# The chunked two-way scan of an RWKV-style mixer: its triangular inverse as a counted loop on TensorE, in four array tiles

## The chip, the core and the metric

One core of one Trainium2 chip runs one program: two layers of a first block and one layer of a second block, all in fp32. The metric is device time in microseconds (us). The kernel before takes 3105.51 us, the median of 3 runs (3105.34 to 3112.76). The profiled execution took 3111.09 us, with a span of 3109.3 us.

## The reference, cut to what matters

The change touches only the recurrence of the second block: 16 heads of 64 channels, two directions (forward and backward in time), 256 context tokens and then 256 tokens of x, the state carried from one to the other.

```python
def wkv_scan(s0, scan_in):
    def step(s, inp):
        w, kk, a, k, v, r = inp          # decay, removal key, rate, key, value, receptance
        sa = jnp.einsum('dbhij,dbhj->dbhi', s, kk)
        s = s * w[..., None, :] - sa[..., :, None] * (kk * a)[..., None, :] + v[..., :, None] * k[..., None, :]
        return s, jnp.einsum('dbhij,dbhj->dbhi', s, r)
    return lax.scan(step, s0, scan_in)

s_ctx, y_c = wkv_scan(s0, scan_c)        # context: only the state is used
_, y_x = wkv_scan(s_ctx, scan_x)         # x: the outputs are used
```

## The kernel before

**Chunks.** The scan goes in 8 steps of 64 tokens, 4 of context and 4 of x. In a step both directions run side by side, so there are 32 chains (16 heads, 2 directions). A buffer such as `Pm`, `Qm` or `LT` is 128 x 1024: its two partition halves are the two heads of a pair, and its columns are 2 directions x 8 pairs x 64. Inside a chunk the recurrence is solved with 64x64 matrices. `Qm` and `Pm` are the decayed removal keys, `Km` the decayed keys, `Rm` the receptances. `LT` is their masked product, `Apk`, `Arq` and `Ark` are the other masked products, and `Kt`, `Qt` and `VT_TOK` are the keys and values turned to token-major by a product with the identity.

**The inverse.** The inverse of the unit triangular matrix and its transpose are held in `Dm` and `DTm` and grow by doubling blocks (level masks for block sizes 1, 2, 4, ... 32). The first level is made from `LT` and from a second product `L` by masks alone. Five levels follow, each with three products per direction: `AL` = masked left matrix `Loff` times `Dm`, copied out by ACT to `ARm`; `E` and `ET`, which DVE subtracts from `Dm` and `DTm`. DVE also makes the next level's `Loff` from `LT`.

**Products on TensorE.** `product()` (L1623) opens one PSUM bank per direction, waits for its operands and issues 8 pairs x 2 heads matmuls of 64x64 by 64. fp32 makes each of them two weight loads and two matmul instructions. A head reads its own partition half and writes the same half of the bank, so of the four 64x64 tiles of the array only the two on the diagonal are used, in turn. One direction of one product, here called a bank, is 32 matmul instructions.

**Order.** `head()` (L1655) makes a step's products and inverse, `tail()` (L1676) the values `U0`, the corrected values `U`, the outputs `Y` (x only) and the state `St`. Each engine runs its own program, in order. PSUM goes through two rings of 4 banks, one emptied by ACT and one by DVE, and a bank is opened when its last user has freed it. The 8 steps are written as loops on each engine (`pe.Fori(0, 3)` at L1696 for context, `pe.Fori(0, 2)` at L1705 for x) with straight code around them; the PE loop body is a whole step. The next step's rates are made inside the inverse: `rate_sums` on DVE, `sigmoids` (L1913) on ACT, two running sums `cumulate` on DVE (after levels 1 and 2), `decays` (L1918) on ACT, and then six products on DVE for `Qm`, `Pm` and `Km`. GpSimd (POOL) copies two small inputs per step (L2582, L2588). Since two scan buffers lie where x is, x is written to HBM before the scan and read back after it.

Of the kernel before, what the change touches and what calls it, by code (L numbers as in the profile page):

```python
# [13 lines left out]
P = 128  # L14
# [24 lines left out]
def sections(*parts):  # L39

    out, at = {}, 0
    for name, passes, per in parts:
# [6 lines left out]
SECTIONS_ACT = sections(("layers", LAYERS, 92), ("attention", 1, 120), ("scan_first", 1, 16), ("scan_ctx", 3, 20),  # L49
                        ("scan_turn", 1, 20), ("scan_x", 2, 20), ("scan_end", 1, 20), ("scan_last", 1, 4))  # L50
SECTIONS_DVE = sections(("layers", LAYERS, 64), ("attention", 1, 28), ("scan_first", 1, 32), ("scan_ctx", 3, 32),
                        ("scan_turn", 1, 36), ("scan_x", 2, 36), ("scan_end", 1, 32), ("scan_last", 1, 4))
# [74 lines left out]
def constants2():  # L127
# [23 lines left out]
    put("level", np.tile(np.stack(levels, 1), (2, 1, 1, 1)))  # L151
# [105 lines left out]
class PsumRing:  # L257
# [31 lines left out]
    def peek(self, eng, section, tag, k):  # L289

        n = [i for i, t in enumerate(self.filled[section]) if t == tag][k]
        eng.wait_ge(self.full, self.count(section, 0, n))
        return self.banks[:, n % 4, :]

# [26 lines left out]
def build_program(nc, W1, V1, K1, W2_all, VV2, K2, R2, PU, PV, xin, cin, out):  # L321
# [931 lines left out]
    css2, csd2, crs2 = sm2[:, 108:110], sm2[:, 110:112], sm2[:, 112:114]  # L1253
    ys, yd, yr = sm2[:, 120:152], sm2[:, 152:184], sm2[:, 184:216]
# [18 lines left out]
    lor = rb(256).rearrange("p (d s t) -> p d s t", d=2, s=2)  # L1273
# [7 lines left out]
    Z = [sb2(1024, slots_at + 1024 * i) for i in range(14)] + [sb2(1024, 1024 * i) for i in range(2)] + [rb(1024) for _ in range(7)]  # L1281
    assert slots_at + 14 * 1024 <= base - nv2 - ncon2 - ncon and rtop[0] <= MEM_COLS, rtop[0]
    r0, r1, r2, r3, Pm, nU, Rm, ARm, Loff, U0, Qm, Km, Dm, DTm, VT_TOK, _, Kt, Qt, Apk, Ark, Arq, LT, St = Z
# [5 lines left out]
    Vt = r3  # L1289

# [22 lines left out]
    def pb(n):  # L1313
# [62 lines left out]
    shifted_ready, lora_act_ready = signal("shifted_ready"), signal("lora_act_ready")  # L1376
    kk_sq_ready, kk_root_ready, scan_ready = signal("kk_sq_ready"), signal("kk_root_ready"), signal("scan_ready")

    step_in_ready, values_in_ready = signal("step_in_ready"), signal("values_in_ready")
    inputs_used = signal("inputs_used")  # L1380
    lora_sums_ready, rates_ready = signal("lora_sums_ready"), signal("rates_ready")
    cumsum_ready, decays_ready = signal("cumsum_ready"), signal("decays_ready")
    pq_ready, k_ready, r_ready = signal("pq_ready"), signal("k_ready"), signal("r_ready")
    intra_ready, tokens_ready = signal("intra_ready"), signal("tokens_ready")
    level_left_ready, inverse_ready, inverseT_ready = (
        signal("level_left_ready", 10), signal("inverse_ready", 10), signal("inverseT_ready", 12))
    u0_ready, u_ready = signal("u0_ready", 2), signal("u_ready", 2)
    state_ready = signal("state_ready")
    x_back = sem("x_back")
    scan_done_act, scan_done_dve = sem("scan_done_act"), sem("scan_done_dve")  # L1390
# [6 lines left out]
    idx_used = sem("idx_used")  # L1397
# [11 lines left out]
    def _(sp):  # L1409
        sp.dma_start(rows2, R2.rearrange("p (m n) -> p m n", m=2)).then_inc(rows_landed, 16)  # L1410
        sp.dma_start(ctxs, cin.rearrange("(t p) n -> p t n", p=P)).then_inc(ctx_landed, 16)
        for n, (name, count) in enumerate(ITEMS2):
            if n == LAST_BEFORE_SCAN + 1:

                sp.wait_ge(shift_parts_ready.sem, 1)
                sp.dma_start(lora, W2[:, w2_total:w2_total + 2048]).then_inc(lora_landed, 16)

                sp.wait_ge(*xn2_ready.at(0, 0))
                sp.dma_start(out.rearrange("(t p) n -> p t n", p=P), x).then_inc(stored, 16)
                sp.wait_ge(scan_done_act, 1)  # L1420
                sp.wait_ge(scan_done_dve, 1)
            if n == LAST_BEFORE_SCAN + 3:
                sp.wait_ge(stored, 16)
                sp.dma_start(lora[:, 0:1024], W2[:, w2_total + 2048:w2_total + 3072]).then_inc(lora_landed, 16)
                sp.dma_start(x, out.rearrange("(t p) n -> p t n", p=P)).then_inc(x_back, 16)
# [12 lines left out]
        sp.wait_ge(stored, 48)  # L1438
# [3 lines left out]
    def _(pe):  # L1442
# [163 lines left out]
        def stand():  # L1606

            pe.sem_inc(pe_step, 1)

        def section(name):  # L1610
            act_ring.pe_section = dve_ring.pe_section = name

        def operand(buf, head, chain):

            rows_ = slice(64 * head, 64 * head + 64)
            if buf is None:
                return ident[rows_, rows_]
            return ch(buf)[rows_, chain, :]

        def product(ring, it, tag, *terms, ready=None):  # L1620


            for d in range(2):  # L1623
                b = ring.open(pe, it, tag)
                if ready is not None:
                    for r in ready(d):
                        pe.wait_ge(*r)
                stand()
                for c in range(8):
                    for head in range(2):  # L1630
                        for i, (lhsT, rhs) in enumerate(terms):
                            last = mm(b[64 * head:64 * head + 64, c * 64:(c + 1) * 64], operand(lhsT, head, 8 * d + c),
                                      operand(rhs, head, 8 * d + c), i == 0, i == len(terms) - 1, skip=True)
                last.then_inc(ring.full, 1)

        def rates(it, h):

            pe.wait_ge(*step_in_ready.at(h))
            stand()
            for d in range(2):  # L1640
                for c in range(8):
                    if c % 4 == 0:
                        b = dve_ring.open(pe, it, "lora")
                        stand()
                    last = mm(b[:, (c % 4) * P:(c % 4 + 1) * P], lora[:, d * D + c * P:d * D + (c + 1) * P],
                              lor[:, d, :, :].rearrange("p s t -> p (s t)"), True, True)
# [987 lines left out]
```

## Time and profile before

| | |
|---|---|
| median of 3 runs | 3105.51 us |
| profiled execution, its span | 3111.09 us, 3109.3 us |
| busy: PE, DVE, ACT, POOL | 2772.7, 1450.2, 571.7, 333.4 us |
| mean granted TensorE clock | 0.941 |
| 64x64 matmul instructions in the scan | 14080, 444.3 us |
| the scan, from its last setup memset to its last state product | 1690 to 2217 us |

A step of the scan can be timed by any instruction that comes once in it. A row of groups gives busy time, the mean duration of one instruction, and the idle time of the engine before them with what ended it. A row of windows gives each engine's busy time and instruction count in a stretch, and the clock granted to TensorE (1.0 is 2.4 GHz, 0.5 is 1.2 GHz).

### The profile page before, as it was taken

How to read it: one execution, taken by the hardware profiler on the slowest of the kernel's cores; microseconds unless marked ns; L12 is line 12 of the kernel's file. 1: busy time of each engine (PE TensorE's matmuls, PEld its weight loads, DVE VectorE, ACT ScalarE, POOL GpSimd, SP SyncE). 2: the span in 40 equal slices, each digit the busy share in tenths (PEclk: the TensorE clock that was granted, in tenths of full speed). 3: DMA queues.
4: the chain of work that ended last, by engine and by line, in shares of the span. 5: the costliest groups of instructions: out<-in, count | busy, mean ns of one | idle time of the engine just before them, and what ended most of it. 6: DMA issues, size and time to landing. Idle time of an engine off the chain costs nothing.

```text
span 3109.3 us, 54722 instructions
## 1 busy us (share of the span) xinstructions
PE 2772.7 (89%) x22658; PEld 1942.1 (62%) x22658; DVE 1450.2 (47%) x3078; ACT 571.7 (18%) x1254; POOL 333.4 (11%) x310
## 2 busy tenths in 40 slices
PE   8997799899978998999996899999898887878777
PEld 6786586477865853444686898989785633333332
DVE  2635200135352001054363777777412687777754
ACT  1241100013320000114222333222100211111111
POOL 0000000000000000000000000000000255444452
PEclk9998999998989999999998999999999999898898
DMA  4322243242223344313420000000333699999996
GB/s 182 136 82 85 105 163 149 108 177 107 86 82 125 146 162 179 142 72 119 154 94 1 4 4 4 4 4 4 130 136 122 263 422 421 421 421 422 421 421 287
DMA packets 55639, 510.22 MB, mean 164 GB/s; under 512 B 6112, under 2 KB 6112, under 8 KB 8032
## 3 DMA queue, kind: packets, MB, share of 16 engines
q0 software_dynamic: 37024, 269.12, 20.9%
q1 hardware_dynamic: 18368, 237.51, 20.0%
q8 instruction: 191, 3.13, 0.4%
q14 instruction: 56, 0.46, 0.0%
HBM read 504.51 MB, written 2.10 MB: 163 GB/s over the span
## 4 chain that ended last, share of the span: by engine, by line
PE 31%; DMA 11%; DVE 7%; PEld 5%; issue 3%; ACT 1%; DVEq 1%; POOL 0%; PEldq 0%; ACTq 0%; POOLq 0%; SPq 0%
PE psum L1453 28%; DMA mem<-weights,mem 11%; PEld psum L1453 5%; DVE mem L2522 3%; PE psum L1792 2%; DVE mem L2027 2%; DMA mem<-weights 1%; POOL mem L2601 0%; PE psum L1463 0%; ACT mem L2012 0%; ACT mem L2007 0%; DVE mem L2450 0%; DVE mem L2483 0%; DVE mem L2442 0%; DVE mem L2444 0%
## 5 line engine op out<-in xcount | busy, mean ns | idle before, releaser
L1453 PE MATMUL psum<-mem 64*64 64x64 f32 (+5 forms) x16792 | 1120.0, 253 | 93.8 <-issue 39.8
L517 PE MATMUL psum<-mem 128*128 128x256 f32 (+8 forms) x4228 | 1067.5, 421 | 25.6 <-DVE mem L1174 12.9
L1453 PEld LDWEIGHTS psum<-mem 64*64 64x64 f32 (+3 forms) x16792 | 887.3, 145 | 322.1 <-issue 244.5
L517 PEld LDWEIGHTS psum<-mem 128*128 128x128 f32 (+3 forms) x4228 | 769.2, 196 | 317.1 <-issue 227.1
L1792 PE MATMUL psum<-mem 128*128 128x512 f32 x1024 | 507.0, 655 | 134.2 <-ACT mem L2012 133.9
L1792 PEld LDWEIGHTS psum<-mem 128*128 128x128 f32 x1024 | 210.3, 210 | 430.2 <-issue 252.1
L2601 POOL DMA_INDIRECT mem<-weights,mem x256 | 313.0, 1223 | 610.5 <-PE psum L1792 289.3
L2522 DVE CUSTOM_DVE_ANT_0 mem<-mem 128x1024 f32<-128x1024 f32 x256 | 307.9, 1224 | 145.3 <-DMA mem<-weights,mem 140.0
L2027 DVE TENSOR_TENSOR mem<-mem 128x512 f32<-128x512 f32 (+4 forms) x378 | 268.3, 727 | 119.2 <-ACTq L1848 82.7
L2027 DVE TENSOR_TENSOR mem<-psum,mem 128x512 f32<-128x512 f32 (+3 forms) x178 | 99.0, 585 | 175.9 <-PE psum L1453 156.3
L1908 ACT ACTIVATE mem<-psum 128x512 f32<-128x512 f32 x160 | 95.5, 597 | 341.3 <-PE psum L1453 341.3
L2027 DVE TENSOR_TENSOR mem<-mem,psum 128x512 f32<-128x512 f32 x148 | 101.5, 687 | 63.2 <-PE psum L1453 49.2
L2582 POOL COPY mem<-mem 64x64 f32 x32 | 9.5, 298 | 1088.7 <-DVEq L2224 1081.8
L1198 DVE TENSOR_TENSOR mem<-mem 128x512 f32<-128x512 f32 x32 | 22.2, 693 | 202.9 <-ACTq L914 202.9
L535 PE MATMUL psum<-mem 128*128 128x128 f32 (+2 forms) x390 | 55.7, 304 | 67.5 <-DVEq L1152 33.9
L994 DVE SCALAR_TENSOR_TENSOR mem<-mem 128x256 f32<-128x256 f32 x240 | 105.6, 481 | 10.5 <-issue 1.8
L2007 ACT ACTIVATE mem<-mem 128x4 f32<-128x4 f32 x64 | 13.1, 205 | 506.9 <-DVE mem L2526 506.9
L1202 DVE TENSOR_TENSOR mem<-psum,mem 128x512 f32<-128x512 f32 x8 | 5.5, 692 | 212.9 <-PE psum L517 212.9
L535 PEld LDWEIGHTS psum<-mem 128*128 128x128 f32 (+2 forms) x390 | 50.3, 152 | 74.8 <-issue 72.9
L2012 ACT ACTIVATE mem<-mem 128x128 f32<-128x128 f32 x256 | 81.8, 390 | 29.9 <-DVE mem L2027 29.4
L776 ACT ACTIVATE mem<-psum 128x512 f32<-128x512 f32 (+5 forms) x94 | 48.5, 570 | 108.2 <-PE psum L517 102.9
L1212 POOL DMA_DIRECT2D mem<-vectors x2 | 1.3, 646 | 607.8 <-DVEq L1203 606.9
(218 smaller groups left out, 1037.4 us busy)
## 6 DMA issues: line engine op xcount, KB each, us to landing
mem<-weights SPq DMA_DIRECT2D x102, 2048.0 KB, 7.3
mem<-weights SPq DMA_DIRECT2D x2, 2176.0 KB, 7.9
mem<-weights,mem POOLq DMA_INDIRECT x256, 22.2
mem<-weights SPq DMA_DIRECT2D x2, 1536.0 KB, 7.5
mem<-weights SPq DMA_DIRECT2D x3, 1024.0 KB, 9.3
mem<-weights SPq DMA_DIRECT2D x2, 1152.0 KB, 8.1
mem<-weights SPq DMA_DIRECT2D x2, 1120.0 KB, 5.1
mem<-x SPq DMA_DIRECT2D x1, 1024.0 KB, 5.9
```

The source lines that it names most:

```text
L517: ins = pe.matmul(out, lhsT, rhs, start=start, stop=stop, skip_group_check=skip)
L535: last = pe.transpose(b[0:rows_, at:at + n], src, ident[0:n, 0:n])
L776: return A(dst, src(b) if src else b, func).then_inc(act_ring.free, 1)
L994: v.scalar_tensor_tensor(cacc[:, c, :], src, w, cacc[:, c, :], ALU.mult, ALU.add)
L1198: v.tensor_tensor(f, f, f, ALU.mult).then_inc(ff_ready.sem, 1)
L1453: ins = pe.matmul(out, lhsT, rhs, start=start, stop=stop, skip_group_check=skip)
L1792: last = pe.matmul(psum[:, 4 + 2 * t + half, :], diag[:, n % DIAGS, :], rows_uv[n % NBUF][:, D + half * 512:D + (half + 1) * 512], start=k ...
L1908: done(A(dst[:, d * 512:(d + 1) * 512], take(tag, it), ACT.Copy, scale=scale))
L2012: A(diag[:, n % DIAGS, :], ident, ACT.Copy, scale=g1[:, n:n + 1]).then_inc(diag_ready.sem, 1)
L2027: return v.tensor_tensor(o, a, b, op)
L2522: v.tensor_tensor_reduce(u, u, h2[:, t, :], 1.0, 0.0, ALU.mult, ALU.add, actp[:, n:n + 1])
L2601: pool.indirect_dma_start(out=rows_uv[n % NBUF], out_offset=None, in_=UV, in_offset=bass.IndirectOffsetOnAxis(ap=eidx_u[:, n:n + 1], axis= ...
```

## The change

The steps are written out on every engine; the outer loops go. What is a loop now is the inverse, on TensorE alone: six turns, one per level, for each of the 8 steps. The other engines' code for the six levels is written out.

Let h be the step. The left matrix is no longer masked before the product: `LT` minus the identity (subtracted by POOL) is multiplied by `Dm` in all six levels, and DVE puts the level's mask (now minus the mask, with the diagonal kept) on the product as it leaves PSUM. The new `Dm` and `DTm` are then plain products, copied out of PSUM. They begin as identities, and the `L` product goes. Operands and results now change partition halves, so that the two products of a level fall on all four array tiles.

```diff
+        def tile(b, d, c, head, swapped_in, swapped_out, lhsT, rhs, first=True, last=True):
+            side, out = head ^ swapped_in, head ^ swapped_out
+            return mm(b[64 * out:64 * out + 64, c * 64:(c + 1) * 64], lhsT(side, d, c), rhs(side, d, c), first, last, skip=True)
...
+            with pe.Fori(0, LEVELS) as j:
+                for d in range(2):
+                    pe.wait_ge(inverse_ready.sem, j * 2 + ((2 * LEVELS - 2) * h + d + 1))
...
+                            last = tile(left[d], d, c, head, 0, 1, half_of(LT), half_of(Dm))
+                    last.then_inc(left_full.sem, 1)
+                for d in range(2):
+                    pe.wait_ge(left_ready.sem, j * 2 + (2 * LEVELS * h + d + 1))
+                    pe.wait_ge(inverseT_ready[d].sem, j + ((LEVELS - 1) * h + 1))
...
+                            one = tile(products[d][0], d, c, head, 1, 0, half_of(DTm), half_of(ARm))
+                            two = tile(products[d][1], d, c, head, 1, 1, half_of(ARm), half_of(DTm))
+                    one.then_inc(inverse_full.sem, 1)
+                    two.then_inc(inverseT_full.sem, 1)
```

On DVE and ACT, per level (`between` is where the next step's rates go: `cumulate` after levels 0 and 1, with the wait for the sigmoids in front of the first):

```diff
+            for j in range(LEVELS):                      # DVE
+                for d in range(2):
+                    v.wait_ge(*left_full.at(h, 2 * j + d))
+                    tt(dir_(ARm, d), left[d]..., bc(level[:, j, 1 - d, :], 1, 8), ALU.mult)
+                    v.drain().then_inc(left_ready.sem, 1)
+                if j < LEVELS - 1:
+                    v.wait_ge(*inverseT_full.at(h, 2 * j + 1))
+                    v.tensor_copy(DTm[:, 512:1024], banks)
+                    v.drain().then_inc(inverseT_ready[1].sem, 1)
+                between(j)
...
+                        if j == 0:
+                            v.wait_ge(*rates_ready.at(h + 1))
+                        cumulate(j)
+                    if j == 1:
+                        exclude()
...
+            for j in range(LEVELS):                      # ACT
+                for d in range(2):
+                    if j < LEVELS - 1:
+                        act.wait_ge(*inverse_full.at(h, 2 * j + d))
+                        A(Dm[:, d * 512:(d + 1) * 512], banks[2 * d], ACT.Copy)
+                        act.drain().then_inc(inverse_ready.sem, 1)
+                    if j == LEVELS - 1 or d == 0:
+                        act.wait_ge(*inverseT_full.at(h, 2 * j + d))
+                        A(DTm[:, d * 512:(d + 1) * 512], banks[2 * d + 1], ACT.Copy)
...
+                between(j)          # j == 0: sigmoids(h + 1); 2: first_decays(h + 1); 3: later_decays()
```

The key products become 128 columns wide: one weight load of `Qm` (or `Km`) meets `Pm` and the identity in one matmul, giving `LT` and `Qt` (or `Apk` and `Kt`). Two of them with different tiles are interleaved (`together`). `U0`, `Y` and `St` are cut into phases that put terms of the two directions on different tiles; between phases PE waits for its own last matmul (`term_full`). `Ark` and `Arq` are interleaved in the same way. The rates are two products with 64 rows each instead of one with 128.

```diff
+        def wide(bank, d, c, head, swapped_out, lhsT):
+            out = head ^ swapped_out
+            to = bank[64 * out:64 * out + 64, :].rearrange("p (b n) -> p b n", b=2)[:, :, 64 * (c % 4):64 * (c % 4) + 64]
+            return mm(to, lhsT(head, d, c), removal_and_unit(head, d, c), True, True, skip=True)
...
+        for h in STEPS:
+            read = h - 1 in X_STEPS
+            if read:
+                y = first_outputs(h - 1)
+            else:
+                together(removal(h, 0))
+            if h:
+                corrected_values(h - 1)
+            if read:
+                last_outputs(h - 1, y)
+            if h:
+                state_update(h - 1)
+            values_product(h)
...
+            together(removal(h, 1), keys(h, 0))          # where not read; where read: both directions in pairs
+            together(keys(h, 1))
+            pe.wait_ge(*qt_ready.at(h, 1))
+            if h < 7:
+                for d in range(2):
+                    rates(h + 1, d)
+            uncorrected(h)
+            if h in X_STEPS:
+                reads(h)
+            inverse(h)
```

`Qm`, `Pm` and `Km` are now made by POOL, with a two-instruction form of the key factor:

```diff
+                pool.wait_ge(*rates_ready.at(h + 1))
...
+                removal_raw(h + 1)      # Qm = kk * r1                 (2 products of 128x512)
+                key_factors()           # r1 = r1 * k_a + (1 - k_a)    (4)
+                removal_keys(h + 1)     # waits decays_ready; Qm *= r2 (128x1024), Pm = kk * r3 (2); then pq_ready
+                keys_raw(h + 1)         # r1 *= zk                     (2)
+                keys(h + 1)             # Km = r1 * r2 (128x1024); then k_ready
```

After the last step the state is no longer updated. Two fewer scan buffers are needed, so x stays in place and its trip to HBM and back goes.

## Rows read from the trace of the kernel before

**Rows 1.** Windows, the whole core: five steps of the scan, then their columns.
```profile
core 0: us, PE busy (x) PEld busy (x) DVE busy (x) ACT busy (x) POOL busy (x), PEclk, DMA share, GB/s
1793.00:1852.84 59.84, 54.51 (x1639) 53.42 (x1636) 43.01 (x68) 19.46 (x27) 2.09 (x6) 0.94 0.02 4
...
1913.70:1974.65 60.95, 58.13 (x1768) 56.11 (x1765) 46.82 (x74) 19.36 (x26) 2.46 (x6) 1.00 0.02 4
1974.65:2041.38 66.73, 63.63 (x1956) 61.82 (x1954) 48.33 (x76) 19.36 (x27) 2.09 (x6) 1.00 0.02 4
```

**Rows 2.** Groups by shape in 1670 to 2215 us, all engines.
```profile
L1453 PE MATMUL psum<-mem 64*64 64x64 f32 x14080 | 444.3, 221 | 46.1 <-issue 39.8 <-DVE mem L2027 2.7
...
L2027 DVE TENSOR_TENSOR mem<-mem,psum 128x512 f32<-128x512 f32 x144 | 99.0, 687 | 63.2 <-PE psum L1453 49.2 <-issue 8.4 <-PEq L1688 1.0
L1908 ACT ACTIVATE mem<-psum 128x512 f32<-128x512 f32 x160 | 95.5, 597 | 341.3 <-PE psum L1453 341.3
...
L2027 DVE TENSOR_TENSOR mem<-mem 128x1024 f32<-128x1024 f32 x31 | 38.1, 1229 | 3.7 <-issue 1.3
...
L2272 DVE TENSOR_TENSOR_SCAN mem<-mem 128x512 f32<-128x512 f32 x16 | 19.5, 1223 | 6.5 <-ACT mem L1915 3.5 <-issue 2.1
L1915 ACT ACTIVATE mem<-mem 128x2048 f32<-128x2048 f32 x8 | 15.3, 1911 | 0.1
```

**Rows 3.** Timeline of ACT: the table load that comes once per step (start, duration).
```profile
1737.05 1.28 ACT L1915 ACT_TABLE_LOAD   x1 [0.18 <-issue]
1791.69 1.28 ACT L1915 ACT_TABLE_LOAD   x1 [0.25 <-issue]
...
1973.36 1.28 ACT L1915 ACT_TABLE_LOAD   x1 [0.18 <-issue]
2040.09 1.28 ACT L1915 ACT_TABLE_LOAD   x1 [0.24 <-issue]
```

**Rows 4.** Timeline of one level: an evacuation, then PE's first weight load after it.
```profile
1922.68 0.60 ACT L1908 ACTIVATE mem<-psum 128x512 f32<-128x512 f32 x1 [4.58 <-PE psum L1453]
...
1923.63 0.69 PEld L1453 LDWEIGHTS psum<-mem 64*64 64x64 f32 x20 [0.19 <-issue]
```

**Rows 5.** Windows: 64x64 products, the rates, and narrow products in the first block.
```profile
1902.00:1905.50 3.50, 3.50 (x128) 3.50 (x124) 2.96 (x6) 2.39 (x4) 0.00 (x0) 1.00 0.02 5
1905.67:1909.20 3.53, 3.53 (x35) 3.53 (x32) 2.67 (x8) 0.60 (x1) 0.00 (x0) 1.00 0.02 5
...
173.54:173.80 0.26, 0.26 (x18) 0.26 (x18) 0.26 (x1) 0.15 (x1) 0.00 (x0) 1.00 0.45 189
```

**Rows 6.** Groups by shape in 173.4 to 174.3 us: the narrow products.
```profile
L517 PE MATMUL psum<-mem 128*15 128x64 f32 x16 | 0.5, 222 | 0.0
```

**Rows 7.** Loop lines of PE (L1696) and DVE (L2363): duration least, median, most.
```profile
L1696 PEldq COMPARE_BRANCH  x3: 83/3360/3378, 1818.2 to 1939.0; - x3
...
L2363 DVEq COMPARE_BRANCH  x3: 50/67/74, 1819.0 to 1939.9; - x3
```

**Rows 8.** Windows around the first taken branch of the context loop on PE.
```profile
1817.40:1822.00 4.60, 0.16 (x6) 0.05 (x2) 1.74 (x5) 3.32 (x4) 0.00 (x0) 0.74 0.01 4
1822.00:1824.00 2.00, 2.00 (x37) 2.00 (x39) 1.80 (x4) 0.00 (x0) 0.00 (x0) 0.50 0.04 8
...
1826.00:1828.00 2.00, 2.00 (x68) 2.00 (x66) 0.40 (x1) 0.35 (x2) 0.00 (x0) 0.90 0.03 8
```

**Rows 9.** POOL's groups by shape.
```profile
L2588 POOL COPY mem<-mem 128x512 f32 x16 | 9.3, 608 | 433.5 <-DVEq L2315 433.5
```

**Rows 10.** Timeline at both ends of the scan.
```profile
1690.00 0.07 DVE L2219 MEMSET mem<- 128x8 f32 x1
...
1711.11 0.17 DVE L2297 COPY mem<-mem 128x8 f32<-128x8 f32 x1 [4.71 <-ACT mem L1924]
...
1735.33 0.60 ACT L1908 ACTIVATE mem<-psum 128x512 f32<-128x512 f32 x1 [4.26 <-PE psum L1453]
...
2215.53 1.23 DVE L2027 TENSOR_TENSOR mem<-mem 128x1024 f32<-128x1024 f32 x1
```

More of the change, by code:

```diff
@@ L293, in peek, with held @@
         return self.banks[:, n % 4, :]
+    def held(self, count):
+        tags = self.emptied[self.section]
+        tags.extend(["held"] * count)
+        return [self.banks[:, n % 4, :] for n in range(len(tags) - count, len(tags))]
     def check(self, section):
@@ L1605, in _ @@
         pe.wait_ge(*scan_ready.at(0))
[L1606 to L1620, printed above, removed]
-            for d in range(2):
[L1624 to L1628, printed above, removed]
+        act_ring.pe_section = dve_ring.pe_section = "post"
@@ L1634, in product, with corrected_values @@
[L1634 to L1639, printed above, removed]
+                        last = tile(b, d, c, head, 0, 1, values(h), unit)
+                last.then_inc(act_ring.full, 1)
+        def corrected_values(h):
+            for d in range(2):
+                b = act_ring.open(pe, 0, "U")
+                pe.wait_ge(*inverse_done.at(h, d))
+                pe.wait_ge(*u0_ready.at(h, d))
+                for c in range(8):
+                    for head in range(2):
+                        last = tile(b, d, c, head, 1, 0, half_of(DTm), half_of(U0))
+                last.then_inc(act_ring.full, 1)
@@ new lines, in output_terms @@
+        def output_terms(h, b, phases):
+            terms = ((0, half_of(Rm), half_of(St)), (1, half_of(Ark), half_of(VT_TOK)), (0, half_of(Arq), half_of(nU)))
+            for phase in phases:
+                for c in range(8):
+                    for head in range(2):
+                        for d, i in phase:
+                            swapped, lhsT, rhs = terms[i]
+                            last = tile(b[d], d, c, head, swapped, 0, lhsT, rhs, i == 0 and c == 0, i == 2)
+                if phase[-1][1] == 2:
+                    last.then_inc(dve_ring.full, 1)
+                else:
+                    pe.wait_ge(term_full.sem, mark(last))
@@ new lines, in keys, with together @@
+        def keys(h, d):
+            b = [act_ring.open(pe, 0, "K") for _ in range(2)]
+            return lambda c, head: wide(b[c // 4], d, c, head, 1, half_of(Km)), act_ring
+        def together(*products):
+            for c in range(8):
+                for head in range(2):
+                    last = [product(c, head) for product, _ in products]
+                if c % 4 == 3:
+                    for ins, (_, ring) in zip(last, products):
+                        ins.then_inc(ring.full, 1)
@@ L1640, in rates, with reads @@
+        def reads(h):
+            b = [[dve_ring.open(pe, 0, n) for n in ("Arq", "Ark")] for _ in range(2)]
             for d in range(2):
                 for c in range(8):
[L1642 to L1646, printed above, removed]
@@ L1959, in _ @@
+        corrected_values()
+        act.sem_inc(scan_done, 1)
         act.wait_ge(*y_var_ready.at(0))
```

584 lines of the change are left out of this document (328 added, 256 removed).

## The prediction

> **What bounds the kernel now.** The slices and the chain of waits on the page say that PE is busy nearly everywhere; outside the scan the change moves only one transfer. So I read the scan alone: windows by step, groups by shape, then the timeline of one level. PE's records cover 63.6 of 66.7 us of a step of x [rows 1], but a busy PE is not a full one. The dense row holds 128 matmul instructions in 3.50 us, 27 to 29 ns each [rows 5] (records missing or cut at the edges allow both; I use 29.2, and 0.93 us for a bank of 32). A context step without a taken branch takes 54.64 us, a step of x 66.73 [rows 3]. A context step has 50 banks (12 in the head, 28 in the inverse, 10 in the tail): 46.7 us. Its rates are 32 instructions of 128 columns, 3.53 us [rows 5]. Together 50.2 of 54.6 us: PE's instruction stream is the bound, hand-offs cost 4.4 us a step. DVE is busy 43 to 48 us and ACT 19 [rows 1]; both wait for PE [rows 2].
>
> **Array tiles.** Each 64x64 instruction takes 2 x 29.2 = 58 ns of its tile, and two tiles alternate. Do four go at once? No 64x64 product shows it, but narrow ones do: 18 instructions in 0.26 us, 14.4 ns each [rows 5], nearly all of one kind, 64 moving columns into 15 output partitions [rows 6], which go to four column groups in turn. That is four times the rate of one tile. I take 14.6 ns for products on four tiles. Bounds: 14.6, and 29.2 if the row halves or the issue don't allow it.
> The Trainium skill, TensorE: Matmul & The Clock Gate (Back-to-back issue gap), says that matmuls never start less than about 25 ns apart on average. The short burst above goes below it, but 18 instructions can come out of a queue, and no row shows a long run. By that rule four tiles give 25 and not 14.6: a rival below.
>
> **A level of the new inverse.** Left products: 2 banks on two tiles, 1.87 us. Two products per direction on four tiles: 64 instructions x 14.6 = 0.93, both directions 1.87. PE work 3.74 us, six times 22.4, against 28 banks or 26.1 us before. Hand-offs decide instead. From a bank's last matmul to the evacuation I take 0.3 (matmul 0.22 [rows 2] and an estimate of 0.1 for the semaphore); evacuation 0.69 on DVE, 0.60 on ACT [rows 2]; from there to PE's next weight load 0.35 (1922.68 + 0.60 to 1923.63) [rows 4]. One direction: left 0.93 + 1.34 + products 0.93 + 1.25 = 4.45 us. The other fills the gaps, but ACT must copy `Dm`, `DTm` and the other `Dm` in turn, which pushes the second left product some 0.15 late: 4.6 us a level (bounds 3.74, work alone, and 5.1). The register waits and the branch lie under PE's queue. Six levels: 2.3 to the first product + 5 x 4.6 + 2.3 for the last pair = 27.6.
>
> **What the next step's rates add (steps 0 to 6).** After level 0 DVE waits for the sigmoids before its first running sum, and level 1's masks stand behind that wait. ACT finishes level 0's copies about 5.5 us into the inverse, then table load 1.28 [rows 3] and sigmoids 1.91 [rows 2]: 8.9; running sum 1.22 and mask 0.69 [rows 2], hops: PE goes on at 11.3, where it would at 6.9. That is 4.4 us with PE idle. Before, the sum stood one level later and waited for nothing. After level 1: second sum 1.22, difference 1.23 [rows 2], hops, less 0.5 of slack: 2.2. The clock: when PE stood 4.6 us at a taken branch, the granted clock went from 1.0 to 0.50 and stayed there until about 1827 [rows 8]. The new gap is as long. Most of the work behind it is hand-offs, so I charge 1.0 (0 to 3.4). Sum 7.6; the inverse takes 35.2, in step 7 27.6.
>
> **Head and tail of a context step, from the last product on.** The wide products are 64 matmuls, 128 instructions of twice the length: 32 on two tiles 1.8, 64 on four 1.8, 32 on two 1.8. `U` 1.9. State: 0.93 + 0.93 on four tiles + 0.93, with two waits for its own last matmul of 0.4 (0.22 and issue): 3.6. Values 1.9. Then a stall: `qt_ready` of direction 1 comes behind ACT's other copies and DVE's two masks (`lt`, `Apk`): 1.8. Rates 3.5: I expect no gain from the split, since each instruction still loads 128 columns (bounds 1.8, 3.6). `U0` in phases 3.7. The inverse opens all four held banks first, and waits for `U0`'s copies: 1.3. `inverse_begun`, `k_ready` and the rest are early. With 0.3 for gaps: 23.6. A context step is 58.8, against 54.64 before. So the work falls, and the time doesn't.
> With outputs (steps 5 to 7): `Y` 3.7 + 1.9 with two short waits, less the first wide product (now paired), `Ark`/`Arq` on four tiles 1.9 for 3.7 before, which also hide the 1.3: 28.5. A step of x is 63.7 against 66.73.
>
> **POOL.** It shows no product of two tensors; its copy of 128x512 takes 0.608 [rows 9], DVE's product 0.69. I take 1.2 for one (twice the copy, two operands to read; bounds 0.7 and 2.4), a row between. Behind the sigmoids 6 such, then it waits for the decays (28 us into the inverse, ACT after level 3), 4 more, `pq_ready` at 33, before PE asks at 35.2; 4 more, `k_ready` at 38, PE asks at 44. Hidden by 2 us. What DVE sheds (six products and the identity arithmetic, some 12 us a step) was not on the path.
>
> **Branches.** A taken branch of the big PE loops costs 3.36 us [rows 7], PE stands some 4.5 us and then runs at half clock [rows 8]. The step with one that rows 1 show took 59.84 us, 5.2 more than the 54.64 without; there are three in the scan, 16 us in all, and they go. The new loop has 40 taken branches over about 400 instructions, where the old body has 3400. DVE's loop of about 150 branches back in 0.07 [rows 7]. I take the new ones as free; the other end is 3.4 each.
> The Trainium skill, Runtime: NRT & Kernel Launch (Instruction fetch mechanics), says that PE's instruction memory holds 2048 instructions, and a taken branch outside the window of pages held fetches. That agrees with the rows for both old loops; the same section speaks of two pages of 256 only, which 400 instructions would overrun. That is a rival below.
>
> **The sum.** The scan before: 1690.1 to 2216.8, 526.7 us [rows 10]. After: start 43 (decays ready 21.0 after its start [rows 10], 1.7 less for POOL's copies, then 8 POOL products 9.6 and the head of 14; before, the first `AL` ended at 45.2), seven inverses 246.4, one 27.6, heads and tails 4 x 23.6 = 94.4, 3 x 28.5 - 3.5 (no rates in step 7) = 82.0, `Ark`/`Arq` in step 4 0.6, last outputs 9.3. Sum 503.3: 23.4 less. The write and read of x lay beside other work (0 to 1): nothing. Against the profiled execution: 3111.1 - 23.4 = 3087.7. It is 5.6 above the median of the runs, so I predict 3082.
>
> **Rivals.**
> - *Four tiles run no faster than two* (chance 0.10). Level 5.9 and not 4.6, the wait behind the sigmoids stays, +9.7 per inverse and +7.9 in the last, heads +3.7 and +6.5: 110 more, 3192, slower. For: no row has row and column tiles at once. Against: rows 5 and 6.
> - *The taken branch refetches* (0.10): 40 x 2.9 (3.4 less what queue and hand-off hide) = 116: 3198, slower. It decides from 0.6 us a branch. Against it stand the small loops [rows 7], on another engine.
> - *An issue floor near 25 ns* (0.13): four-tile phases 1.6 and not 0.93, level 5.2, 28 more in 47 levels, heads 8: 3118. The page named above has this rule.
> - *POOL is late* (0.10): at 2.4 a product `pq_ready` comes 2.3 late, `k_ready` 2.6: 18 more, 3100.
> - *Hand-offs overlap as well as before* (0.12): then PE's work sets the step, 22.4 + 18.2 + 4.4 = 45 us; 13.8 less in 8 steps: 2972. For: before, 4.4 a step was all they cost. Against: there three products a level gave cover, and the sigmoid wait is in the code's order. Half of it gives 3027.
> - *Forecast* (0.45): 3082, own range 3050 to 3118.
>
> **Chances.** Below 0.3% (about 9 us) this measurement can't tell a change. Faster: 0.39 of the forecast, 0.12 overlap, 0.03 each of POOL and the floor: 0.57. Same: 0.13 (0.03, 0.06 POOL, 0.04 floor). Slower: 0.30, the two large rivals, the rest of the floor, the edge of the others. The range 3010 to 3190 leaves out half of each large rival and of the fast one.
>
> **What would show it.** The ACT table load every 59 to 64 us; in a level four-tile groups of 64 matmul instructions in about 0.93 us; left products about 4.6 us apart, and after level 0 PE idle some 4.4 us with DVE waiting for the sigmoids, and a clock of 0.5 behind it. PE busy falls, though the span hardly does. POOL busy rises by some 200 us. Wrong would be: COMPARE_BRANCH rows of microseconds in the inverse (refetch), 1.6 or 1.9 us for four-tile groups, `pq_ready` ending PE's idle time, or rates in 1.8 us.

## The result, and the profile after

The changed kernel takes 3113.57 us, the median of 16 runs (3104.33 to 3119.65), against 3107.84 (3104.29 to 3112.76) before: 1.0019 times, 95% interval [1.0011, 1.0028]. It is 6 us slower, less than the 0.3% below which the prediction calls two kernels the same. Forecast were 3082 and, with a chance of 0.57, faster. The profiled execution has a span of 3117.7 us.

The page of after: busy time by engine. PE is 57 us less busy than before, DVE 146 less, and POOL 165 more.
```profile
PE 2715.8 (87%) x23298; PEld 1882.3 (60%) x23298; DVE 1304.0 (42%) x2811; ACT 605.9 (19%) x1310; POOL 498.2 (16%) x390
```

Windows of after: the whole scan; a context step, the step that ends in the first head of x, and a step of x (each from the sigmoids' table load to the next one's); then a head of context and a head of x. Columns as in [rows 1], which the middle three answer to.
```profile
1690.00:2229.00 539.00, 428.07 (x14976) 408.83 (x14976) 220.53 (x305) 190.64 (x265) 182.05 (x128) 0.87 0.01 2
...
1808.05:1865.34 57.29, 46.04 (x1733) 44.01 (x1728) 24.71 (x34) 23.67 (x33) 22.69 (x16) 0.97 0.01 2
1927.43:1988.20 60.77, 47.92 (x1844) 45.61 (x1842) 28.27 (x40) 23.67 (x33) 22.68 (x16) 0.97 0.01 2
1988.20:2060.05 71.85, 59.23 (x2071) 56.62 (x2067) 30.44 (x43) 23.67 (x34) 22.68 (x16) 0.86 0.01 2
...
1777.30:1802.30 25.00, 22.03 (x582) 20.96 (x576) 8.13 (x12) 6.57 (x11) 8.70 (x7) 0.86 0.01 3
...
2019.70:2053.60 33.90, 29.43 (x905) 27.94 (x896) 11.99 (x18) 6.57 (x11) 8.88 (x7) 0.85 0.01 3
```
The same view of before:
```profile
1690.00:2217.00 527.00, 475.83 (x14336) 464.16 (x14336) 365.41 (x570) 156.65 (x209) 18.84 (x48) 0.96 0.02 4
```
PE's records cover 48 us less in the scan, and the granted clock went from 0.96 to 0.87: about 44 us at half clock became 140. Between the ends named in [rows 10] the scan takes 537.0 us, for 526.8 before. A context step takes 57 to 62 us where one without a taken branch took 54.64, and this step of x 71.85 for 66.73 [rows 1, 3].

Groups by shape of after, 1670 to 2215 us, as in [rows 2], and the counted loop's instructions, as in [rows 7]:
```profile
L1460 PE MATMUL psum<-mem 64*64 64x64 f32 x12998 | 335.4, 236 | 75.2 <-DVEq L2452 51.3 <-issue 5.5 <-ACT mem L2011 5.2
...
L2705 POOL TENSOR_TENSOR mem<-mem 128x512 f32<-128x512 f32 x96 | 128.9, 1359 | 1295.3 <-ACT mem L2015 1248.6 <-DVEq L2395 42.9 <-issue 1.4
...
L2705 POOL TENSOR_TENSOR mem<-mem 128x1024 f32<-128x1024 f32 x16 | 37.7, 2357 | 94.3 <-ACT mem L2024 93.0
...
L2176 DVE TENSOR_TENSOR mem<-mem 128x1024 f32<-128x1024 f32 x15 | 23.8, 1586 | 1.3
L2433 DVE TENSOR_TENSOR_SCAN mem<-mem 128x512 f32<-128x512 f32 x16 | 23.6, 1479 | 27.3 <-ACT mem L2015 26.5
...
L1765 PEldq COMPARE_BRANCH  x48: 76/208/243, 1744.1 to 2218.8; - x48
```
The loop's branch takes 0.21 us, at most 0.24 in 48 turns, where the old loop's taken branch took 3.36 [rows 7]: the price of a refetch doesn't appear. Beside POOL's products DVE's sums went from 1223 to 1479 ns and its 1024-wide operations from 1229 to 1586 [rows 2].

What PE waits for in the scan of after (us in total, times, longest):
```profile
PE psum L1460 <- DVEq L2452: 51.3, 15, 4.1
PE psum L1460 <- POOLq L2727: 17.9, 1, 17.9
PE psum L1460 <- ACTq L2041: 16.9, 8, 3.2
PE psum L1460 <- DVEq L2371: 9.9, 1, 9.9
```
L2452 is the drain behind DVE's mask (`left_ready`), L2041 the one behind `Qt` (`qt_ready`), L2727 POOL's behind `pq_ready`, which is waited for once, in the start. The timeline of after around level 0 of step 1 shows how the first comes about:
```profile
1808.05 1.28 ACT L2015 ACT_TABLE_LOAD   x1
1809.35 1.91 ACT L2015 ACTIVATE mem<-mem 128x2048 f32<-128x2048 f32 x1
1811.29 1.23 DVE L2433 TENSOR_TENSOR_SCAN mem<-mem 128x512 f32<-128x512 f32 x1 [3.62 <-ACT mem L2015]
1811.33 5.67 POOL L2705 TENSOR_TENSOR mem<-mem 128x512 f32<-128x512 f32 x4 [21.56 <-ACT mem L2015]
1812.43 1.48 DVE L2176 TENSOR_TENSOR mem<-psum,mem 128x512 f32<-128x512 f32 x2
...
1813.36 2.94 PE L1460 MATMUL psum<-mem 64*64 64x64 f32 x101 [4.08 <-DVEq L2452]
```
Level 0's copies end, ACT loads a table and makes the sigmoids, DVE stands 3.62 us for them and makes a running sum, and only then level 1's masks. PE stands 4.08 us.

And after's PE before the next step's rates in step 1's head:
```profile
1790.81 7.06 PE L1460 MATMUL psum<-mem 64*128 64x64 f32 x96 [1.49 <-ACTq L2041]
```
Windows of the stall, of the rates that follow it, and of what comes next:
```profile
1789.00:1790.80 1.80, 0.32 (x6) 0.08 (x2) 0.99 (x2) 1.19 (x2) 0.77 (x1) 1.00 0.00 0
1790.80:1795.60 4.80, 4.79 (x64) 4.79 (x64) 1.29 (x2) 0.60 (x1) 0.00 (x0) 0.73 0.01 3
1795.60:1800.10 4.50, 4.27 (x102) 3.86 (x102) 1.29 (x2) 0.04 (x1) 0.00 (x0) 0.53 0.00 0
```
The 64 instructions of the rates take 4.8 us, and at full clock 3.4 to 3.5 (below, and [rows 5]). The clock is 1.00 in the stall and 0.53 five us behind it. That doesn't follow every such stall: PE stands 1.5 us there in all four heads behind context steps, and the granted clock of the heads behind steps 0 and 2 is 0.86, of those behind steps 1 and 3 it is 1.00:
```profile
1777.10:1802.30 25.20, 22.23 (x595) 21.12 (x586) 8.13 (x12) 6.57 (x11) 8.90 (x7) 0.86 0.01 3
...
1837.40:1859.60 22.20, 19.38 (x603) 18.40 (x594) 8.24 (x12) 6.70 (x12) 9.17 (x7) 1.00 0.02 4
```

### The profile page after: what moved, and what is told of

It is laid out like the page before. It is cut to its first block, busy times and chain, and to the rows that moved or that the text cites. A ratio compares the mean times of both kernels' runs of the same rounds, so it can differ in the third digit from the quotient of the medians.

```text
span 3117.7 us, 55234 instructions
## 1 busy us (share of the span) xinstructions
PE 2715.8 (87%) x23298; PEld 1882.3 (60%) x23298; DVE 1304.0 (42%) x2811; ACT 605.9 (19%) x1310; POOL 498.2 (16%) x390
## 4 chain that ended last, share of the span: by engine, by line
PE 31%; DMA 11%; DVE 8%; PEld 4%; ACT 2%; issue 2%; DVEq 1%; POOL 1%; POOLq 0%; ACTq 0%; PEldq 0%; SPq 0%
PE psum L1460 28%; DMA mem<-weights,mem 11%; PEld psum L1460 4%; DVE mem L2654 3%; PE psum L1895 2%; DVE mem L2176 2%; DVE mem L2433 1%; DMA mem<-weights 1%; ACT mem L2015 0%; POOL mem L2783 0%; PE psum L1470 0%; ACT mem L2036 0%; ACT L2015 0%; POOL mem L2705 0%; ACT mem L2070 0%
## 5 line engine op out<-in xcount | busy, mean ns | idle before, releaser
L1460 PE MATMUL psum<-mem 64*64 64x64 f32 (+6 forms) x17432 | 1070.2, 268 | 151.4 <-DVEq L2452 51.3
L1460 PEld LDWEIGHTS psum<-mem 64*64 64x64 f32 (+3 forms) x17432 | 830.5, 157 | 386.4 <-issue 266.9
L1895 PE MATMUL psum<-mem 128*128 128x512 f32 x1024 | 499.7, 647 | 141.9 <-ACT mem L2161 141.9
L2783 POOL DMA_INDIRECT mem<-weights,mem x256 | 314.6, 1229 | 583.9 <-PE psum L1895 288.3
L2705 POOL TENSOR_TENSOR mem<-mem 128x512 f32<-128x512 f32 (+1 forms) x112 | 166.3, 1502 | 1389.6 <-ACT mem L2015 1248.6
L2176 DVE TENSOR_TENSOR mem<-psum,mem 128x512 f32<-128x512 f32 (+1 forms) x224 | 150.9, 685 | 326.9 <-PE psum L1460 308.7
L2176 DVE TENSOR_TENSOR mem<-mem 128x4 f32<-128x4 f32 (+5 forms) x201 | 148.0, 745 | 105.1 <-ACTq L1951 82.7
L2070 ACT ACTIVATE mem<-psum 128x512 f32<-128x512 f32 x80 | 47.8, 597 | 139.7 <-PE psum L1460 136.9
L2455 DVE COPY mem<-psum 128x512 f32<-128x512 f32 x40 | 27.7, 692 | 81.8 <-PE psum L1460 81.8
```

The lines of the kernel that those rows point to most:

```text
L1460: ins = pe.matmul(out, lhsT, rhs, start=start, stop=stop, skip_group_check=skip)
L1895: last = pe.matmul(psum[:, 4 + 2 * t + half, :], diag[:, n % DIAGS, :], rows_uv[n % NBUF][:, D + half * 512:D + (half + 1) * 512], start=k ...
L2070: A(Dm[:, d * 512:(d + 1) * 512], banks[2 * d], ACT.Copy)
L2176: return v.tensor_tensor(o, a, b, op)
L2705: return pool.tensor_tensor(o, a, b, op)
L2783: pool.indirect_dma_start(out=rows_uv[n % NBUF], out_offset=None, in_=UV, in_offset=bass.IndirectOffsetOnAxis(ap=eidx_u[:, n:n + 1], axis= ...
```

## The experiments

Each was timed in 3 rounds (the last in 5) beside the kernel before on the same chip; ratios are to that. Times against the changed kernel use its median of 3113.57. Two measures in the texts below need a word. The half-clock times 119.5 and 47.8 count stretches that began between 1690 and 2240 us, one of 10.2 us behind the scan among them, and leave out the one that was running at its start; over the scan itself they are 140 and 44. The traces begin their scans up to 5 us apart, at 1690.4 us in after and at 1685.1 to 1690.3 in the runs, so what is said below of a whole scan goes from its own memset, though some windows are shown from 1690. "Level" is the time from one loop branch to the next.

**1. Sigmoids and sums ahead of level 0.** On ACT `sigmoids(h + 1)` goes ahead of the copies of `U0`; on DVE both sums go ahead of the first mask:
```diff
+            if h < 7:
+                v.wait_ge(*rates_ready.at(h + 1))
+                cumulate(0)
+                cumulate(1)
             def next_rates(j):
                 if h < 7:
-                    if j in (0, 1):
-                        if j == 0:
-                            v.wait_ge(*rates_ready.at(h + 1))
-                        cumulate(j)
-                    if j == 1:
+                    if j == 0:
                         exclude()
```


> Edit on the changed kernel: ACT takes the next step's sigmoids before it copies U0, and DVE both running sums before the first level of the inverse, the difference after level 0. Nothing is left out. Theory (waits behind the sigmoids and the second sum): in the trace after, level 1 of an inverse takes 9.8 us and level 2 some 8 to 9, where the later levels take 4.4 to 4.5; that is about 9.5 us in each of 7 steps, 66 us. The sums now cost about 1.5 us ahead of the first mask, so 50 to 60 us less than the changed kernel, about 3055 us, and the half-clock stretches inside the inverses go. Rival (PE is held by a low clock and hand-offs wherever the sums stand): the wait only moves ahead of level 0, and less than 20 us are won.

Measured: 3076.76 us, 0.9907 [0.9889, 0.9925], 37 less than the changed kernel, short of the 50 to 60 expected. Levels 1 and 2 of a context step went from 9.8 and 8.9 us (step 0) to 5.8 and 4.4, and the context inverses from 35 to 37 us to 27.5 to 27.9. In steps of x they took 33. There DVE's sums now stand behind the masks of `Arq` and `Ark`, and in front of level 0's mask (DVE's timeline, step 4):
```profile
1949.18 2.48 DVE L2176 TENSOR_TENSOR mem<-psum,mem 128x512 f32<-128x512 f32 x4 [3.99 <-PE psum L1460]
1951.80 3.98 DVE L2433 TENSOR_TENSOR_SCAN mem<-mem 128x512 f32<-128x512 f32 x2
1955.71 1.47 DVE L2176 TENSOR_TENSOR mem<-psum,mem 128x512 f32<-128x512 f32 x2
```
The two sums take 3.98 us, for 2.45 at the duration of [rows 2]: POOL works beside them. The stall after level 0 was as predicted; that it could be had back everywhere was not true of x. And the four heads behind context steps grew from 96.5 to 102.8 us together: the granted clock of the first two is 0.81 here (windows 1765.00:1791.40 and 1819.00:1845.80), for 0.86 and 1.00 in after.

**2. The rates wait for their own direction only**, and ACT makes `Qt` of direction 1 before `Kt` of direction 0:
```diff
-            pe.wait_ge(*qt_ready.at(h, 1))
-            if h < 7:
-                for d in range(2):
+            for d in range(2):
+                pe.wait_ge(*qt_ready.at(h, d))
+                if h < 7:
                     rates(h + 1, d)
...
-            key_tokens(h, 0)
             removal_tokens(h, 1)
+            key_tokens(h, 0)
             key_tokens(h, 1)
```


> Edit on the changed kernel: the rates of direction 0 wait for direction 0's Qt copy only, and ACT makes direction 1's Qt copy before direction 0's Kt copy. Nothing is left out. Theory (the wait ahead of the rates and the half clock behind it): PE stands 1.5 to 3.5 us there per step, and in most steps the rates then run at half clock, 6.8 us for 3.4. 20 to 30 us less than the changed kernel, about 3088. Rival (what comes after is bound by DVE's state and sums, so the gap moves to U0): under 8 us less.

Measured: 3081.54 us, 0.9917 [0.9900, 0.9933], 32 less. L2041 is gone from PE's waits, and the head and tail run as one piece, at a granted clock of 1.00 (PE's timeline, then a window that overlaps this stretch):
```profile
1759.80 23.90 PE L1460 MATMUL psum<-mem 64*64 64x64 f32 x816
```
```profile
1763.60:1787.40 23.80, 22.27 (x743) 21.26 (x739) 9.79 (x16) 7.17 (x12) 11.92 (x10) 1.00 0.02 3
```
PE waited 16.9 us for L2041, and 32 came back. The heads of x fell from 34.0, 35.4 and 27.7 to 27.1, 26.3 and 27.0. The stalls after levels 0 and 1 stayed (50.7 us in 15), yet the half-clock time fell from 140 to 72. The context heads tell the wait from the clock: the two that had run at 1.00 became 1.3 and 1.8 us shorter, about their wait of 1.5, and the two that had run at 0.86 became 4.7 and 4.0 shorter. In those two the clock cost some 3 us beside the wait.

**3. The two products of a direction one after the other**, so that only two tiles work at a time:
```diff
                             one = tile(products[d][0], d, c, head, 1, 0, half_of(DTm), half_of(ARm))
+                    for c in range(8):
+                        for head in range(2):
                             two = tile(products[d][1], d, c, head, 1, 1, half_of(ARm), half_of(DTm))
```


> Edit on the changed kernel: inside a level the 16 products for Dm are issued first and the 16 for DTm after them, so that only two of the four array tiles alternate. Nothing is left out. Theory (four tiles give a product pair in 0.95 us and two in 1.87): a level goes from 4.45 to about 5.7, 48 levels, 50 to 60 us more than the changed kernel, about 3170. Rival (hand-offs bound a level, and the pair lies in their cover): 10 to 25 us more. Rival (four tiles are worth nothing): no difference.

Measured: 3158.58 us, 1.0161 [1.0144, 1.0178], 45 more. An undisturbed level went from 4.45 to 5.43 us. In the traces the eight inverses take 321.4 us for 285.4: the levels behind DVE's waits, 1 and 2, grew by 0.4 and 0.2 on average, levels 0, 3 and 4 by 0.6 to 1.0, and the last by 1.5. So the four tiles do run at once, and outside those waits what they save is on the path. A window of version 7 (below) holds one level's two pairs of products, 128 instructions, 15 ns each:
```profile
1838.15:1840.10 1.95, 1.92 (x128) 1.95 (x128) 0.57 (x1) 0.62 (x2) 0.00 (x0) 1.00 0.00 0
```

**4. The six levels written out on PE** (`pe.Fori(0, LEVELS)` becomes `range(LEVELS)`).

> Edit on the changed kernel: the six levels are written out on PE and not a counted loop. Nothing is left out. Theory (the taken branch of 0.2 us lies in PE's waits, and instructions arrive in time): within 5 us of the changed kernel. Rival (branch and register waits cost 0.2 to 0.3 us in each of 48 levels): 10 to 14 us less. Rival (straight code at 15 ns an instruction is held up by instruction fetch, which the loop avoids): 15 us or more above it, with gaps inside the four-tile groups.

Measured: 3158.15 us, 1.0152 [1.0133, 1.0172], 45 more; my theory falls, and what the fetch rival foretold is seen. PE's timeline in a written-out level:
```profile
1891.62 3.20 PE L1460 MATMUL psum<-mem 64*64 64x64 f32 x127 [0.32 <-issue]
1895.55 3.29 PE L1460 MATMUL psum<-mem 64*64 64x64 f32 x126 [0.73 <-issue]
1899.45 2.19 PE L1460 MATMUL psum<-mem 64*64 64x64 f32 x127 [0.61 <-issue]
1903.24 2.98 PE L1460 MATMUL psum<-mem 64*64 64x64 f32 x111 [1.60 <-issue]
```
Every 127 matmuls (with their weight loads about 254 instructions) PE stands with nothing to wait for, the longer the faster the stretch before went: 1.60 us behind 127 in 2.19. Such waits sum to 36.8 us in 49, against 5.7 in 14 with the loop, and the page counts 188 packets (MB, share) of the instruction queue where after had 127:
```profile
q8 instruction: 188, 3.08, 0.4%
```
The times of these packets tie the two together. In the scan each holds 16384 bytes; the ones of this stretch end at 1894.13, 1898.00 and 1901.87 us, and PE goes on at 1895.55, 1899.45 and 1903.24, each time 1.4 us later. So PE waits for its instructions. Written out, the levels lose what the four tiles win (experiment 3): here the loop is what makes the tiles pay.

**5. The same stall, but filled**: 40 idle matmuls before the rates, no hand-off moved.
```diff
+                pe.wait_ge(*qt_ready.at(h, 0))
+                rates(h + 1, 0, fill=h)      # opens its two banks, 40 matmuls into them,
+                rates(h + 1, 1)              # then waits for qt_ready.at(h, 1)
```


> The changed kernel with 40 idle matmuls (64 columns, 2.3 us at full clock) put where PE stands before the next step's rates, into banks that the rates overwrite. No hand-off is moved and no wait is shorter. In the changed kernel PE ran 119.5 us of the scan at half clock, before the change 47.8. Theory A (the half clock behind this gap is a cost by itself, beside the gap): half-clock time in the scan falls below 75 us, the rates behind the gap take 3.4 and not 6.8 us in most steps, and the kernel is 15 to 25 us faster than the changed one: about 3093. Rival B (the clock falls because of the gaps after levels 0 and 1, and the gap before the rates costs only its own length): half-clock time stays at 100 to 120 us, and the time is 3113, or up to 7 more where the fill is longer than the gap.

Measured: 3114.61 us, 1.0016 [1.0006, 1.0025], 1 more. Windows of its whole scan and of its next head:
```profile
1690.00:2221.00 531.00, 441.60 (x15518) 423.52 (x15517) 217.26 (x302) 189.32 (x264) 182.03 (x128) 0.90 0.01 2
...
1771.60:1796.50 24.90, 23.65 (x676) 22.74 (x667) 8.21 (x12) 6.61 (x12) 9.07 (x7) 1.00 0.01 3
```
The clock of this head is 1.00 now, and it takes 24.9 us as before (25.0 at 0.86). Over the scan the half-clock time fell from 140 to 106 us; in the measure of the text above, from 119.5 to 85, which neither theory had. Head by head: those behind steps 0 and 2 kept their length, those behind steps 1 and 3, whose clock was full already, grew by 3.1 and 3.0 us, and the first two of x shrank by 3.4 and 3.9. So standing still does pull the clock down, but 560 idle instructions (23858 on the page, for 23298) cost as much as the clock gives back. A fill buys nothing here; a removed wait can pay twice.

**6. Experiments 1 and 2 together.**

> Both repairs at once: sigmoids before the copies of U0 and both running sums before the first mask, and rates that wait only for their own direction's qt_ready. Alone they were worth 37 and 32 us against the changed kernel. Theory A (two separate places, gaps after the levels and the gap before the rates): the gains add up, 69 less than the changed kernel, about 3045. Rival B (both pay back the same half-clock time, so that the second finds it gone): 3060 to 3070.

Measured: 3039.35 us, 0.9780 [0.9763, 0.9796], 74 less; 37 + 32 is 69. They add up. Half-clock time in the scan is 41 us, for 44 before.

**7. The sums also ahead of the masks of `Arq` and `Ark`**, on top of 6.
```diff
             if h < 7:
                 rate_sums()
+                v.wait_ge(*rates_ready.at(h + 1))
+                cumulate(0)
+                cumulate(1)
             if h in X_STEPS:
```


> As the last one, with the two running sums also ahead of the masks of Arq and Ark in steps 4 to 6. There DVE stands 4 us waiting for reads' banks while the sigmoids are done after 2 of them, and level 0 of the inverse still took 9.8, 9.7 and 8.9 us in the run with the sums moved (4.2 in the other steps). Theory: the sums (1.23 each without POOL's products beside them) fill that wait, and level 0 begins 2.5 us sooner in three steps: 7 us less than with the masks first, about 3038. Rival: the masks free the banks that the inverse opens, so what is won is lost again: no difference (within 2 us).

Measured: 3028.94 us, 0.9741 [0.9724, 0.9757], 10 less than 6, which was timed beside it; 7 were expected. The inverses of x went from 33.3, 33.3 and 30.9 us to 28.1, 28.4 and 28.9, the heads behind two of them took 1.8 and 1.4 more. What PE waits for in its scan:
```profile
PE psum L1460 <- POOLq L2726: 17.9, 1, 17.9
PE psum L1460 <- DVEq L2452: 9.3, 11, 1.3
```
The 51.3 us of L2452 are 9.3. A context step and a step of x, as [rows 1]:
```profile
1808.80:1857.70 48.90, 44.72 (x1735) 42.59 (x1730) 25.12 (x34) 23.47 (x33) 23.16 (x17) 1.00 0.01 2
1958.50:2014.80 56.30, 51.36 (x2059) 48.28 (x2052) 28.67 (x42) 23.47 (x34) 20.70 (x17) 1.00 0.01 2
```

**8. The kernel before with PE's two outer loops written out** (`range(3)`, `range(2)`), to price the branches that the change removes.

> The kernel before with PE's two outer loops written out, so that the three taken branches of the scan are gone; nothing else is changed. Theory A (the step with a taken branch took 59.8 us against 54.6 without): 3 x 5.2 = 16 us less than before, about 3092. Rival B (the loops' code had to be fetched once and now each step's has, so instruction fetch holds two-tile code as well): no gain, or slower, 3108 to 3120.

Measured: 3085.52 us, 0.9925 [0.9908, 0.9942], 24 less than before, for 16 in the prediction. Its steps, as [rows 1]:
```profile
1846.52:1901.20 54.68, 52.91 (x1639) 51.75 (x1636) 42.76 (x67) 19.36 (x26) 2.28 (x6) 1.00 0.02 4
1901.20:1960.84 59.64, 56.85 (x1765) 55.56 (x1762) 46.69 (x73) 19.37 (x26) 2.46 (x6) 1.00 0.02 4
1960.84:2024.75 63.91, 62.04 (x1961) 61.13 (x1958) 48.32 (x75) 19.37 (x26) 2.09 (x6) 1.00 0.02 4
```
A step of x takes 63.9 here and took 66.73 in the loop, without a taken branch in either: the loop held time that no single branch shows, and I had priced only the branches. Why is open.

**9. Version 7 with the rates on four tiles** (each product of 128 columns cut in two of 64).
```diff
-                    last = mm(b[part][:, c * 64:(c + 1) * 64], lora[k, d * D + c * P:d * D + (c + 1) * P],
-                              zwa[k, starts(h)[d]:starts(h)[d] + 64], True, True, skip=True)
+                    for half in range(2):
+                        at = d * D + c * P + 64 * half
+                        last = mm(b[part][64 * half:64 * half + 64, c * 64:(c + 1) * 64], lora[k, at:at + 64],
+                                  zwa[k, starts(h)[d]:starts(h)[d] + 64], True, True, skip=True)
```


> The last best version (both repairs, sums first; 3029) with each of the rates' products of 128 columns cut in two of 64, so that the four go on four tiles of the array: 128 instructions for 64. In the changed kernel a step's rates took 3.4 us at full clock (64 instructions, 53 ns each). Theory (instructions on four tiles start 15 ns apart): 1.9 us, 1.5 less in each of seven steps and in the start, 12 less: 3017. Rival (what bounds the rates is not the tile but the hand-off behind them: DVE empties each of the four banks in 0.69 us, 2.8 in all, and the sigmoids wait for the last): 5 less at most, about 3025.

Measured: 3020.86 us, 0.9722 [0.9709, 0.9735], 8 less than version 7, which was timed apart from it. Against the kernel before in each case it is 6 less, and the two intervals overlap, so the times alone hardly carry this step. The traces do: the scan takes 440.3 us for 447.0, and 5.0 of these 6.7 lie in the start. The rates in version 7, then in this one and the stretch behind them:
```profile
1869.20:1872.60 3.40, 3.40 (x64) 3.23 (x60) 1.89 (x4) 2.30 (x4) 1.27 (x1) 1.00 0.02 5
```
```profile
1863.00:1864.90 1.90, 1.90 (x132) 1.90 (x127) 1.60 (x4) 1.41 (x3) 0.54 (x1) 1.00 0.03 9
1864.90:1867.00 2.10, 0.59 (x20) 0.45 (x18) 1.62 (x3) 1.47 (x2) 0.00 (x0) 1.00 0.00 0
```
1.9 us for 3.4, as the theory said; behind it PE stands for most of 2.1 us, and there part of the expected 12 went. This version beats the kernel before by 87 us.

## Why the prediction was wrong

The sum, term by term. The times are read off PE's loop: its counter is set where an inverse begins, and its last branch ends it. The start counts from the last setup memset of each trace.

| term of the sum | predicted | after | experiment 1 | experiment 2 | version 7 |
|---|---|---|---|---|---|
| start | 43.0 | 49.4 | 49.4 | 43.4 | 43.6 |
| eight inverses | 274.0 | 285.4 | 238.2 | 280.5 | 226.1 |
| four heads and tails after context steps, `Ark`/`Arq` of step 4 | 95.0 | 96.5 | 102.8 | 84.7 | 86.0 |
| three of x | 82.0 | 97.1 | 94.5 | 80.4 | 82.6 |
| last outputs | 9.3 | 8.5 | | | |
| scan | 503.3 | 537.0 | 493.3 | 497.5 | 447.0 |

- **A level of the inverse (4.6 us): right.** An undisturbed level takes 4.4 to 4.5 and the inverse of step 7 27.5 (27.6 predicted). Four tiles run at 15 ns an instruction (64 in 0.94 us), and experiment 3 shows what they are worth. The rivals of slow tiles, of the issue floor and of the refetching branch fall. (The last had less for it than it says: 400 instructions are fewer than two pages of 256 hold, and overrun them only where the loop begins late in a page.)
- **The next step's rates (7.6 a step): right in kind, short by 1.7.** The inverses of steps 0 to 6 exceed that of step 7 by 7.7 to 10.9, mean 9.3. Level 1 took 4.1 to 5.3 us more than an undisturbed one, for 4.4, and level 2 3.3 to 5.1 more, for 2.2. I had taken the durations of sum and difference from a trace in which POOL was idle, and the slow clock, which I had at 1.0 us, is in these numbers. In seven steps this is 12 us. Experiment 1 showed the wait to be the cause: without it the context inverses are 27.7.
- **Heads and tails of x (28.5, 28.5, 25.0): the largest miss, 15 us.** The failing step is "Then a stall: `qt_ready` of direction 1 ...: 1.8", with the clock left at full. In the heads of x the stall is 3.1 to 3.2 us, which makes 4 of the 15. Without it the sum had 76.6, and experiment 2, which takes the wait away and has but 3.4 us at half clock in these three, measured 80.4: another 4 are work priced too low. The 7 that are left are, by subtraction, what half clock cost the rates and the products behind the stall, which I had at nothing.
- **Heads and tails of context steps (95.0, measured 96.5): right by luck.** Stall and work together were priced about 4 us high (experiment 2 took 84.7, where the sum less its stalls has 87.8, and the stalls are 1.5, not 1.8), and the half clock, priced at nothing, took some 6. (The items of one head add up to 23.4, not 23.6; that is 0.8 in four.)
- **The start: 6.4 us short, by the same step.** PE got `pq_ready` 25.8 us into it, 3 sooner than in the sum, but from there to the first inverse it took 23.6 us, for 14. It too has the stall before the rates, 1.50 us, and behind it the 192 instructions up to the inverse are slow:
```profile
1716.27 9.27 PE L1460 MATMUL psum<-mem 64*64 64x128 f32 x192 [17.92 <-POOLq L2727]
1727.04 8.05 PE L1460 MATMUL psum<-mem 64*128 64x64 f32 x96 [1.50 <-ACTq L2041]
1735.24 3.66 PE L1460 MATMUL psum<-mem 64*64 64x64 f32 x96 [0.16 <-PE psum L1460]
```
In experiment 2 the first two rows are one of 14.07 us, for 18.82 with the stall, and the third takes 2.37: the whole start is 43.4. The other 3.6 of those 23.6 are work priced too low.
- **Branches: 16 priced, 24 measured** (experiment 8). That sat in the time before, and the sum for after doesn't need it. But it moves where the gain came from: by subtraction, the rest of the change made the kernel 30 us slower, not 7 faster.
- **POOL: right.** A product of 512 columns takes 1.27 (the one in experiment 9's row of version 7) to 1.36 on average, for 1.2, and PE waits for `pq_ready` only in the start. What I left out is the other side: DVE's sums and differences get 20 to 30% longer on average beside it.
- **"Hand-offs overlap as well as before" (2972):** not met, nor half. With the two waits repaired a context step is 48.9 us, where that rival had 45.

So what PE's work lost (48 us in the scan) was given back by two waits that the change put into the order of ACT and DVE, and by the clock behind them. Experiments 6 and 7 show both: the same products in a better order are 85 us faster. In experiment 2 both have a share: 16.9 us of waiting went, and the two heads that had run at 0.86 lost 3 us each beyond it. How much of experiment 1 is wait and how much is clock stays open.

## What to carry to other kernels

When a change makes the bound engine's stream thinner, price each short wait twice: its length, and the work that may follow it at half clock; and take durations of shared work from a stretch where the other engine is busy too. Then look for what stands ahead of the waiting instruction in each engine's program: an activation's table load and a sum moved up by one level were worth more here than twice as many array tiles. Code that is quicker per instruction may want a loop: here the same levels written out lost 45 us.

## What the hardware showed that I had not expected

- Four-tile products go on at 15 ns an instruction for as long as there are any: 64 in 0.94 us in each level, and 132 in 1.90 us in version 9. The Trainium skill, TensorE: Matmul & The Clock Gate (Back-to-back issue gap), gives an issue floor of about 25 ns for up to 64 columns; the trace does not agree for products of 64 x 64 on four tiles.
- Straight code at that rate is held by instruction fetch: gaps of up to 1.6 us every 127 matmuls, most of them ending about 1.4 us after a packet of 16 KB has landed (experiment 4), where the loop's branch of 0.21 us costs nothing. The Trainium skill, Runtime: NRT & Kernel Launch (Instruction fetch mechanics), calls the cost of crossing a block of 256 instructions mostly hidden, and warns of a taken branch whose target lies outside two such blocks. The trace does not agree with the first for this level; and the branch over some 400 instructions, which need not leave two blocks, was cheap.
- Waits of 1.5 to 4 us, about three in a step (23 in the scan), brought the granted clock of the whole scan from 0.96 to 0.87; without most of them it was 0.95 and 0.96, with less work on PE than before (experiments 6 and 7). A single wait of 1.5 us was followed by half clock in two of four context heads, and not in the other two.
- DVE's operations that read two operands from SBUF slow down beside POOL's products: a sum of 512 columns from 1223 ns to 1479 on average and 1.99 each in experiment 1, the difference of 1024 from 1229 to 1586. Instruction by instruction the averages are of two kinds. A sum that began just ahead of POOL's product, as the one at 1811.29 us did by 0.04, took its 1.225 us; one that began while a product was under way took 1.08 us and what was left of that product (1.37 us at 1817.90 with 0.29 left, 1.97 at 1874.59 with 0.89 left). Its evacuations from PSUM kept their 689 ns. The Trainium skill, GPSIMD Engine Reference (Specifications), names this contention for DVE instructions with two inputs in SBUF; the trace agrees, and my prediction left it out.
